# Sparse attention with probabilities and values split into rounded high and low terms, and its three branches added on GpSimd

## What is computed

```python
# for each head h, in words of the reference
o_cmp = softmax(q @ k_cmp.T + bias) @ v_cmp     # 31 compressed keys
o_sel = softmax(q @ k_sel.T + bias) @ v_sel     # the selected keys, up to 512
o_win = softmax(q @ k_win.T + bias) @ v_win     # a window of up to 384 keys
out   = gate0 * o_cmp + gate1 * o_sel + gate2 * o_win
```

## Time and profile before

| | us |
|---|---|
| median of three runs | 2755.93 |
| the profiled execution's own time | 2757.42 |
| span of the profiled execution | 2755.6 |
| PE busy (matmul) | 2711.6 (98%) |
| PE weight loads busy | 2248.7 (82%) |
| DVE (VectorE) busy | 1440.7 (52%) |
| ACT (ScalarE) busy | 1058.5 (38%) |
| POOL (GpSimd) busy | 36.4 (1%) |

### The profile page before, as it was taken

The page is one execution under the profiler, slowest core; times in us unless marked ns, Lnnn a source line. Parts: engine busy times, 40 slices in busy tenths (PEclk is TensorE's granted clock), DMA queues, the critical chain, the costliest instruction groups (busy, mean ns, idle before and its releaser), DMA issues.

```text
span 2755.6 us, 38503 instructions
## 1 busy us (share of the span) xinstructions
PE 2711.6 (98%) x16358; PEld 2248.7 (82%) x16358; DVE 1440.7 (52%) x2360; ACT 1058.5 (38%) x1604; POOL 36.4 (1%) x62
## 2 busy tenths in 40 slices
PE   9988999999999999999999999999999999999998
PEld 7787788888887788888888888877888788888887
DVE  6834576643625756756346443274634544654433
ACT  5534454332425654433234222245433422432221
POOL 0000200000000000000000000001000000000000
PEclk9999999999999999999999999999999999999999
DMA  4200122222531002322323332236222232223222
GB/s 161 90 4 3 53 87 98 100 94 98 158 104 39 1 1 100 100 97 95 100 77 107 99 99 93 100 116 129 82 81 87 71 100 98 87 99 99 93 99 69
DMA packets 68686, 238.85 MB, mean 87 GB/s; under 512 B 7800, under 2 KB 10360, under 8 KB 68004
## 3 DMA queue, kind: packets, MB, share of 16 engines
q1 hardware_dynamic: 62256, 220.80, 23.9%
q10 hardware_dynamic: 6260, 15.59, 2.5%
HBM read 228.23 MB, written 6.03 MB: 85 GB/s over the span
## 4 chain that ended last, share of the span: by engine, by line
PE 91%; DVE 4%; ACT 3%; issue 1%; POOL 1%; DMA 0%; ACTq 0%; another core or an unknown queue 0%; DVEq 0%; POOLq 0%
PE psum L155 23%; PE psum L157 23%; PE psum L156 23%; PE psum L1330 3%; PE psum L1297 2%; PE psum L1317 2%; PE psum L843 2%; PE psum L201 2%; PE psum L202 1%; PE psum L209 1%; PE psum L1851 1%; PE psum L177 1%; PE psum L178 1%; PE psum L176 1%; PE psum L1987 1%
## 5 line engine op out<-in xcount | busy, mean ns | idle before, releaser
L155 PE MATMUL psum<-x_hi,w_hi 128*128 128x512 f32 x2128 | 846.1, 398 | 0.7 <-DVE w_lo L130 0.7
L157 PE MATMUL psum<-x_hi,w_lo 128*128 128x512 f32 x2128 | 830.4, 390 | 0.0
L156 PE MATMUL psum<-x_lo,w_hi 128*128 128x512 f32 x2128 | 829.5, 390 | 0.0
L130 DVE TENSOR_TENSOR w_lo<-raw,w_hi 128x1024 fp32r<-128x1024 f32 x409 | 500.2, 1225 | 391.7 <-ACT w_hi L123 391.6
L123 ACT ACTIVATE w_hi<-raw 128x1024 fp32r<-128x1024 f32 x409 | 427.9, 1050 | 306.0 <-DMA raw<-w_down 83.9
L155 PEld LDWEIGHTS psum<-x_hi,w_hi 128*128 128x128 f32 x2128 | 400.0, 188 | 90.6 <-issue 5.7
L156 PEld LDWEIGHTS psum<-x_lo,w_hi 128*128 128x128 f32 x2128 | 400.2, 188 | 85.5 <-issue 5.0
L157 PEld LDWEIGHTS psum<-x_hi,w_lo 128*128 128x128 f32 x2128 | 399.8, 188 | 83.8
L157 PE MATMUL psum<-h_hi,w_lo 128*128 128x512 f32 x616 | 240.0, 390 | 0.0
L156 PE MATMUL psum<-h_lo,w_hi 128*128 128x512 f32 x616 | 240.0, 390 | 0.0
L155 PE MATMUL psum<-h_hi,w_hi 128*128 128x512 f32 x616 | 240.0, 390 | 0.0
(11 more groups left out here) (412 smaller groups left out, 3298.5 us busy)
## 6 DMA issues: line engine op xcount, KB each, us to landing
raw<-w_up SPq DMA_DIRECT2D x88, 512.0 KB, 3.3
raw<-w_down SPq DMA_DIRECT2D x44, 512.0 KB, 3.3
raw<-w_f1up SPq DMA_DIRECT2D x44, 512.0 KB, 3.3
raw<-w_f2up SPq DMA_DIRECT2D x44, 512.0 KB, 3.3
raw<-w_qkv SPq DMA_DIRECT2D x36, 512.0 KB, 3.3
raw<-w_blend SPq DMA_DIRECT2D x28, 512.0 KB, 3.3
raw<-w_f1down SPq DMA_DIRECT2D x22, 512.0 KB, 3.3
raw<-w_f2down SPq DMA_DIRECT2D x22, 512.0 KB, 3.2
```

What stands on the lines that cost most here:

```text
L130: dve.tensor_tensor(self.w_lo[u % SLOTS][:], self.raw[u % SLOTS][:], self.w_hi[u % SLOTS][:].bitcast(F32), ALU.subtract).then_inc(self.lo_ ...
L155: pe.matmul(bank[:], hi, x_hi[:, kk], start=kk == 0, stop=False)
L156: pe.matmul(bank[:], hi, x_lo[:, kk], start=False, stop=False)
L157: mm = pe.matmul(bank[:], lo, x_hi[:, kk], start=False, stop=kk == kt - 1)
```

## The change

The probabilities' transposes `pt` become fp32r (the copy of ScalarE rounds them), and VectorE writes what the rounding left, `turn bank - pt`, into new buffers `pt_lo` (function `remainders`). The values are split in the same way by GpSimd at the end of `nsa_input`, into `v_hi` and `vt_lo`/`vc_lo`. Each product of line 1330 becomes three: high probabilities by high values, high by low, low by high. The values get a second column of ones (66 columns in place of 65, 132 in place of 130). A turn bank comes free when the remainder is written (`rest`), not when the copy is. In `settle`, VectorE stops after the product into `prod`, now doubled; GpSimd adds the three branches in two additions (`add_branches`). An output bank is free after the product into `prod`; `back_to_features` still waits for `taken`, now given by GpSimd. The sliding-window stage keeps its products.

```diff
@@ paired_attention
-    V = HD + 1
+    V = HD + 1 if mem.pt_lo is None else HD + 2
+    split = mem.pt_lo is not None
...
-            freed.append((copied, c0 + n))
+            freed.append((rest, r0 + n) if split else (copied, c0 + n))
...
             if g >= len(out_bank):
-                pe.wait_ge(taken, g0 + g + 1 - len(out_bank))
+                if steps == 3:
+                    pe.wait_ge(own, o0 + steps * (g + 1 - len(out_bank)))
+                else:
+                    pe.wait_ge(taken, g0 + g + 1 - len(out_bank))
             n = 0
             for c, blocks in enumerate(chunks[p]):
                 pe.wait_ge(copied, c0 + count[(p, c)])
+                if split:
+                    slot = (c0 + count[(p, c)]) % 4
+                    pe.wait_ge(rest, r0 + count[(p, c)])
+                    for j, (_, (v_hi, v_lo), w, at) in enumerate(blocks):
+                        out, cols = out_bank[g % len(out_bank)][:, at * V:at * V + w], slice(j * P, (j + 1) * P)
+                        pe.matmul(out, mem.pt[slot][:, cols], v_hi, start=first_slot[(g, at)] == (p, n), stop=False)
+                        pe.matmul(out, mem.pt[slot][:, cols], v_lo, start=False, stop=False)
+                        mm = pe.matmul(out, mem.pt_lo[slot][:, cols], v_hi, start=False, stop=final_slot[(g, at)] == (p, n))
+                        n += 1
+                    continue
...
+    def add_branches(pool, p):
+        g = parts[p].group
+        prod, ob = mem.prod[g % 2], mem.ob[g % 8]
+        pool.wait_ge(own, o0 + steps * g + 3)
+        pool.tensor_tensor(ob[:], prod[:, 0:P], prod[:, P:2 * P], ALU.add).then_inc(paired, 1)
+        pool.wait_ge(paired, g + 1)
+        pool.tensor_tensor(ob[:], ob[:], prod[:, 2 * P:3 * P], ALU.add).then_inc(taken, 1)
...
-                dve.tensor_tensor(mem.prod[:].rearrange("p (s v) -> p s v", v=HD), view[:, :, 0:HD],
+                if g >= 2:
+                    dve.wait_ge(taken, g0 + g - 1)
+                dve.tensor_tensor(mem.prod[g % 2][:].rearrange("p (s v) -> p s v", v=HD), view[:, :, 0:HD],
                                   coef.unsqueeze(2).to_broadcast([P, n, HD]), ALU.mult).then_inc(own, 1)
-                dve.wait_ge(own, at + 3)
-                dve.tensor_reduce(mem.ob[g % 8][:].rearrange("p (h v) -> p h v", h=2),
-                                  mem.prod[:].rearrange("p (s h v) -> p h v s", h=2, v=HD), AX.X, ALU.add).then_inc(taken, 1)
...
+        def remainders(p):
+            for c, blocks in enumerate(chunks[p]):
+                w, n = len(blocks) * P, count[(p, c)]
+                high = mem.pt[(c0 + n) % 4][:, 0:w]
+                dve.wait_ge(copied, c0 + n)
+                dve.tensor_tensor(mem.pt_lo[(c0 + n) % 4][:, 0:w], turn_bank[place[(p, c)] % 2][:, 0:w], high.bitcast(F32),
+                                  ALU.subtract).then_inc(rest, 1)
...
         for p in range(N + 2):
             if p + 2 < N:
                 mins(dve, p + 2)
+            if split and p < N:
+                remainders(p)
@@ nsa_input, GpSimd
         pool.wait_ge(cleared, 11)
+        pool.wait_ge(kept, 8)
+        wide = 2 * NG * NV
+        tensors = [(mem.vt[t], mem.vt_lo[t], wide) for t in range(TT)] + [(mem.vc, mem.vc_lo, wide // 2)]
+        for n, (full, low, w) in enumerate(tensors):
+            high = mem.v_hi[:, n * wide:n * wide + w]
+            pool.tensor_copy(high, full[:]).then_inc(halves, 1)
+            pool.wait_ge(halves, 2 * n + 1)
+            pool.tensor_tensor(low[:], full[:], high.bitcast(F32), ALU.subtract).then_inc(halves, 1)
@@ nsa_input, done
         eng.wait_ge(valid, 1)
+        eng.wait_ge(halves, 2 * (TT + 1))
```

More of the change, by code:

```diff
@@ L1261, in paired_attention @@
     m0, g0 = k.span("pa_mixed", N), k.span("pa_taken", G)
+    rest, paired = sem("pa_rest"), sem("pa_paired")
+    r0 = k.span("pa_rest", sum(len(c) for c in chunks) if split else 0)
     b0, h0, w0 = (k.span(f"pa_{n}", G // TT) for n in ("back", "high", "lowered"))
@@ L1363, in shift_sinks @@
         pool.tensor_tensor(mem.es[:, i:i + 2], mem.mn[:, i:i + 2], groups[parts[p].group].sinks, ALU.subtract).then_inc(shifted, 1)
+    def add_branches(pool, p):
[5 more added lines that the diff above has]
+        pool.tensor_tensor(ob[:], ob[:], prod[:, 2 * P:3 * P], ALU.add).then_inc(taken, 1)
     def pool(pool):
         if not sinks:
+            for p in range(N):
+                if parts[p].last:
+                    add_branches(pool, p)
             return
@@ L1523 @@
 NG, NH = 4, 16
+NV = HD + 2
 NC = (T - 32) // 16 + 1
@@ L1541, in nsa_input @@
         sem(f"nsa_{n}") for n in ("hidden", "opened", "made", "kept", "gates_turned", "gates_open", "valid", "cleared"))
-    posed = sem("nsa_posed")
+    posed, halves = sem("nsa_posed"), sem("nsa_halves")
     moved = [sem(f"nsa_moved{j}") for j in range(2)]
@@ L1671, in pool @@
         for half in range(2):
-            ones = mem.vc[half * 32:half * 32 + 32].rearrange("p (a h v) -> p a h v", a=2, h=2)[:, :, half, HD:HD + 1]
+            ones = mem.vc[half * 32:half * 32 + 32].rearrange("p (a h v) -> p a h v", a=2, h=2)[:, :, half, HD:NV]
             pool.memset(ones, 1.0).then_inc(cleared, 1)
@@ L1714, in nsa, with values, compressed @@
 def nsa(k, z, mem, opening, ready, sem, head):
-    V, least = HD + 1, 3.0e38
+    V, least = NV, 3.0e38
     groups, parts = [], []
+    wide = 2 * NG * V
+    def values(b, at):
+        return mem.v_hi[:, b * wide + at:b * wide + at + V], mem.vt_lo[b][:, at:at + V]
+    def compressed(at):
+        return mem.v_hi[:, TT * wide + at:TT * wide + at + 2 * V], mem.vc_lo[:, at:at + 2 * V]
     for pair in range(2):
@@ L1736, in nsa @@
                         at = (2 * pair + half) * V
-                        selected_blocks.append(((half, b * P), mem.vt[b][:, at:at + V], V, 2 + half))
-                local_blocks.append(((0, 0), mem.vc[:, pair * 2 * V:(pair + 1) * 2 * V], 2 * V, 0))
+                        selected_blocks.append(((half, b * P), values(b, at), V, 2 + half))
+                local_blocks.append(((0, 0), compressed(pair * 2 * V), 2 * V, 0))
                 for half in range(2):
@@ L1741, in nsa @@
                         at = (NG + 2 * pair + half) * V
-                        local_blocks.append(((half, P + b * P), mem.vt[w0 + b][:, at:at + V], V, 4 + half))
+                        local_blocks.append(((half, P + b * P), values(w0 + b, at), V, 4 + half))
                 parts.append(Part(len(groups), selected_scores, selected, selected_blocks, False))
@@ L2212, with attention_buffers @@
     pass
-def attention_buffers(mem, name, stack, sb):
+def attention_buffers(mem, name, stack, sb, dt=F32):
     mem.p = [[sb(f"{name}_p{j}{half}", [P, T], stack=stack) for half in range(2)] for j in range(4)]
-    mem.pt = [sb(f"{name}_pt{j}", [P, T], stack=stack) for j in range(4)]
+    mem.pt = [sb(f"{name}_pt{j}", [P, T], dt, stack) for j in range(4)]
     mem.ob = [sb(f"{name}_ob{j}", [P, P], stack=stack) for j in range(8)]
     mem.sm = [sb(f"{name}_sm{j}", [P, 16], stack=stack) for j in range(2)]
-    mem.prod = sb(f"{name}_prod", [P, 6 * HD], stack=stack)
+    mem.prod = [sb(f"{name}_prod{j}", [P, 6 * HD], stack=stack) for j in range(2 if name == "nsa" else 0)]
 def shape_constants():
@@ L2340, in build @@
                 attention_buffers(S, "swa", s2, sb)
+                S.pt_lo = None
             L0.rs = [L0.b[:, j:j + 1].rearrange("p a n -> p (a n)") for j in range(4)]
@@ L2379, in build @@
         with ExitStack() as s:
+            with ExitStack() as s2:
+                rounded = sb("z1_rounded", [P, 21, T], F32R, s2)
+            N.pt_lo = [rounded[:, ZKC + j] for j in range(4)]
+            N.v_hi = rounded[:, ZVS:ZVW + 1].rearrange("p a n -> p (a n)")
             z1 = sb("z1", [P, 21, T], stack=s)
-            N.gates, N.keys, N.vc = sb("nsa_gates", [P, TT, 3 * NH], stack=s), sb("nsa_keys", [P, 2, NC + T + NC], stack=s), sb("nsa_vc", [P, NG * (HD + 1)], stack=s)
+            N.gates, N.keys = sb("nsa_gates", [P, TT, 3 * NH], stack=s), sb("nsa_keys", [P, 2, NC + T + NC], stack=s)
+            with ExitStack() as s2:
+                N.vc_lo = sb("nsa_vc_lo", [P, NG * NV], F32R, s2)
+            N.vc = sb("nsa_vc", [P, NG * NV], stack=s)
             N.mn = sb("nsa_mn", [P, 192], stack=s)
-            N.vt = [sb(f"nsa_vt{t}", [P, 2 * NG * (HD + 1)], stack=s) for t in range(TT)]
+            with ExitStack() as s2:
+                N.vt_lo = [sb(f"nsa_vt_lo{t}", [P, 2 * NG * NV], F32R, s2) for t in range(TT)]
+            N.vt = [sb(f"nsa_vt{t}", [P, 2 * NG * NV], stack=s) for t in range(TT)]
             N.table = sb("nsa_table", [P, 7 * P + TT * NC], stack=s)
             with ExitStack() as s2:
-                attention_buffers(N, "nsa", s2, sb)
+                sb("nsa_to_a_line", [P, 56], stack=s2)
+                attention_buffers(N, "nsa", s2, sb, F32R)
             with ExitStack() as s2:
```

4 lines of the change are left out of this document (2 added, 2 removed).

## The result

Four runs of the changed kernel took 2810.44, 2845.85, 2848.55 and 2848.85 us, median 2847.2, against 2756.06 before (four runs, 2755.87 to 2757.27). The ratio by the measurement's own comparison is 1.0295, interval 1.0255 to 1.0334; by the medians it is 1.033. The kernel is 91 us slower, where 41 was forecast, and it no longer has one time. Six more runs of the same kernel, taken later, went from 2811.5 to 2866.8, median 2856, against 2757.7 before on the same chip (1.036 by the medians). The measurement's own comparison leaves out the three slowest of the six, 2866.1 to 2866.8, and gives 1.0262, interval 1.0223 to 1.0302.

A forecast was written before the change was run, and what follows sets the result against it. TensorE's queue was taken as the bound, its products bound by loading the probabilities. 36.3 us for products plus 8 x (0.4 + 0.2) gave +41.1 on the median 2755.9, so 2797.0 us; range 2778 to 2812.

The forecast's parts named there:

- The direction and the bound: Stage that changes: TensorE's queue is the critical path at 21.5 us a cycle; chance of slower by over 0.2%: 0.90.
- The products' price: Line 1330's products: each bound by its 128-column load, 0.108 us; 1008 records in place of 672, +36.3 us.
- VectorE's sum: Remainders add 7.7 us a cycle, reductions removed save 2.4; VectorE goes from 15.1 to 20.4, covered by TensorE's 26.0.
- VectorE's loop at s2: Turn bank freed by the remainder: TensorE some 0.4 us late at s2 once a cycle, bounds 0 and 1.0.
- GpSimd's hand-over: Line 1341 waits for GpSimd's two additions, 0.46 us each: wait 0.36 to 0.5 for 0.24, +0.2 us a cycle.
- The splitting of the values: GpSimd's copies and subtractions from 821.4: 11.9 us, done at 833.3, hidden with 18 us to spare.
- The step that failed: Stage's products: TensorE taken at full granted clock, second column of ones priced at nothing under the load.

The follow-up runs named there:

- the run with fp32 products: Changed kernel with one fp32 product of rounded probabilities and values in place of three fp32r products, all else kept: 2763.4 us, ratio 1.0019.
- padded kernel: Changed kernel, selected and window products widened from 66 to 132 columns into a spare part of the output bank: 2796.6 us; only one of three widened: 2794.9 us.
- the one with a padded product in three: Changed kernel with only the first of a block's three products at 132 columns, the other two at 66: 2794.9 us, 2793.9 to 2795.4.
- GpSimd's additions alone: Kernel before, with GpSimd's two additions in place of VectorE's reduction and the earlier release of the output bank: 2760.2 us, ratio 1.0014.

## Why the prediction was wrong

- **The direction and the bound.** Right. TensorE's queue is the chain in the stage, before and after, and an increase in its records came out as time.
- **The products' price.** Right. Forecast 0.108 us from start to start by the load in line 178; measured 0.111 (898.39 to 898.72 is three distances). Two fp32r records cost the same as two fp32 records. The Trainium skill's about 81 ns for a pair (TensorE: Matmul & The Clock Gate, Back-to-back issue gap), which I didn't take, would have given 1008 x 0.081 = 82 us, an estimate; the trace shows 1008 x 0.111 = 112.
- **VectorE's sum.** Mis-sized. Forecast 15.1 + 5.3 = 20.4 us a cycle, measured 19.0: a remainder overlaps a little with its neighbours, and its row of 700 ns is not what it adds. It was covered either way.
- **VectorE's loop at s2.** Mis-sized in this kernel. The +0.4 us a cycle isn't there: TensorE has no wait for a remainder among its waits, and 8 cycles of 26.25 are 8 x (26.25 - 21.53) = 37.8 us more than before, of which the additional loads alone give 336 x 0.111 = 37.3. With only two records a block it is there (2.6 us in all, in the run with fp32 products).
- **GpSimd's hand-over.** Right: 0.46 us an addition as on the line between the rows, a wait of 0.49 in the forecast 0.36 to 0.5. In the padded kernel's waits it is 2.8 us in 6 times, 0.47 each, for 0.24 before, which over the stage is the forecast 1.6 us. In the kernel before, alone, it costs 3.1 us (waits of 4.8 for 1.7), twice that.
- **The splitting of the values.** Right, hidden: 5.3 + 3.7 + 0.8 + 0.4 = 10.2 us of GpSimd, forecast 11.9, done before 833.
- **The step that failed** is the one that isn't in the sum. I wrote that TensorE runs "at full granted clock" and "the second column of ones costs nothing, as it lies under the load", and carried the clock of the kernel before over to the new one without a term, a bound or a rival. All of the sum's terms together hold: 2755.9 + 37.8 = 2793.7 at full clock, and the padded kernels give 2794.9 and 2796.6, against 2797 forecast. The fall of the clock adds 17 us to the best execution and 53 to the median, and the range ended at 2812. In its place the runs showed a stage at a mean clock of 0.93 and, in another execution, 0.73, where 66 columns in each of three products are run, and of 1.00 with 132 in one of them. The rows to see the risk by were there: 28 ns of columns in a distance of 108 for the new product and 53 for the old, by the durations of 256 and 512 columns. That this would lower the clock was in no row, since the clock was full in every stretch of the stage; that it could should have been a rival. The Trainium skill says (TensorE: Matmul & The Clock Gate, What's actually happening) that the throttled state is the default and activity releases it, and knows two levels, 1.2 and 2.4 GHz. The trace agrees as far as the levels: stretches stand at 0.50 or at 1.00, and the values between are windows that hold both.

## What to carry to other kernels

Where a product is bound by loading its stationary operand, splitting it into more products of a cheaper type multiplies the loads and gained nothing here; count loads first, and look for the form with the fewest. Then look how many columns run under each load, because long runs of narrow products can cost the clock, and a matmul that is "busy" by its record doesn't show it: read the granted clock of each stretch, and read it in several executions. Where the clock falls, try more columns under the same loads: here they brought it back, and the wider products cost no time of their own that these runs can tell.

## What the runs showed of the hardware that I had not expected

- The clock of TensorE fell with TensorE 100% busy by its records (4.00 of 4.00 us in 898 to 902, at a mean clock of 0.71). At 0.50 the distance of load-bound products is 0.213 us against 0.111: the load slows with the clock.
- Useless columns made a kernel 59 us faster (2797 against 2856), and widening a third of the products did it as well as widening all.
- How often the clock falls differs between executions of one program, which spread over 56 us (2810.4 to 2866.8), while no other kernel's runs on one chip spread over more than 9 us (1.6 us for the one with a padded product in three, 8.8 for GpSimd's additions alone).
- Over the span the kernels with one narrow product a block showed a clock of 0.998 or 0.999, the one with two 0.995 to 0.999, and the one with three 0.970 to 0.993; the kernel before showed 0.997 to 0.999.
- In this stage, in three profiled executions, the four long falls came behind the runs of 21 and 24 narrow products, and the three short ones at a transposition that had waited 0.49 to 0.71 us for GpSimd. Why the fall comes in one cycle and not in the next, and in one execution more than in another, stays open.
